# Expert result rows kept in DRAM and added once per token, and the next item's rows transposed inside the down product

## The reference, cut to what matters

```python
def moe_swiglu(a, router, w_gate, w_up, w_down):
    top_v, top_i = lax.top_k((a @ router).astype(jnp.float32), TOP_K)      # TOP_K = 2
    top_w = jax.nn.softmax(top_v, axis=-1)
    gate = jnp.sum(jax.nn.one_hot(top_i, N_EXPERTS) * top_w[..., None], axis=-2)
    out = jnp.zeros_like(a)
    for e in range(N_EXPERTS):                                            # 8
        h = jax.nn.silu(a @ w_gate[e]) * (a @ w_up[e])                    # 1024 -> 1408
        out = out + gate[..., e:e + 1] * (h @ w_down[e])                  # 1408 -> 1024
    return out
```

## Time and profile before

| | |
|---|---|
| median of 3 runs | 1282.21 us (1279.64 to 1285.29) |
| profiled execution | 1278.62 us, span 1276.7 us |
| PE busy | 1191.6 us, 93% of the span |
| DVE, ACT, POOL busy | 471.1, 282.0, 205.0 us |
| expert part | about 841 to 1240 us of the span |
| HBM read and written | 319.16 MB, 15.70 MB |

### The profile page before, as it was taken

How to read it: one execution, slowest core, us unless ns; L and a number is a source line. 1 busy time by engine, 2 the same in 40 slices (tenths; PEclk the granted TensorE clock), 3 DMA queues, 4 the chain that set the end, 5 groups by cost and what they waited for, 6 DMA issues and landing times.

```text
span 1276.7 us, 37806 instructions
## 1 busy us (share of the span) xinstructions
PE 1191.6 (93%) x15722; PEld 981.8 (77%) x15722; DVE 471.1 (37%) x1367; ACT 282.0 (22%) x757; POOL 205.0 (16%) x344
## 2 busy tenths in 40 slices
PE   7999999999999998998786879989899999999998
PEld 5887886999999976675344547787878977878976
DVE  2110114677774332003757674233211311212213
ACT  1000003110010022134867763121010110110122
POOL 3022132021340000223444541010000000000000
PEclk9999999999999998998989899999999999999999
DMA  9786869998443374564556876499999999989831
GB/s 308 294 321 244 316 242 336 152 392 306 139 159 116 149 280 149 169 105 132 182 178 222 263 232 237 158 387 385 399 363 379 360 360 379 349 341 380 318 124 37
DMA packets 109644, 330.06 MB, mean 259 GB/s; under 512 B 15816, under 2 KB 34201, under 8 KB 107812
## 3 DMA queue, kind: packets, MB, share of 16 engines
q1 hardware_dynamic: 91156, 263.86, 56.5%
q0 software_dynamic: 17168, 63.50, 16.3%
q10 hardware_dynamic: 1152, 0.30, 0.1%
HBM read 319.16 MB, written 15.70 MB: 262 GB/s over the span
## 4 chain that ended last, share of the span: by engine, by line
PE 86%; DVE 5%; issue 3%; ACT 2%; DMA 2%; POOLq 0%; POOL 0%; ACTq 0%; DVEq 0%
PE bank L1975 20%; PE bank L2591 15%; PE bank L2077 12%; PE pbank L2602 6%; PE bank L2113 6%; PE bank L2031 5%; PE pbank L2591 3%; PE bank L2602 3%; PE bank L2181 2%; DMA gring<-in_moe 1%; PE bank L2543 1%; PE bank L2208 1%; PE bank L2348 1%; PE bank L2303 1%; PE pbank L2543 1%
## 5 line engine op out<-in xcount | busy, mean ns | idle before, releaser
L2591 PE MATMUL bank<-X,gring 128*64 128x96 f32 x4608 | 197.0, 247 | 5.5 <-issue 5.5
L2591 PEld LDWEIGHTS bank<-X,gring 128*64 128x64 f32 x4608 | 193.0, 138 | 10.1 <-issue 10.1
L1975 PE MATMUL bank<-aT,gring 128*128 128x288 f32 x768 | 193.0, 410 | 3.5 <-DVE aT L1306 3.5
L1975 PEld LDWEIGHTS bank<-aT,gring 128*128 128x128 f32 x768 | 146.6, 192 | 46.2 <-issue 5.6
L2602 PE MATMUL pbank<-Q,X 128*32 128x256 f32 x1152 | 75.3, 379 | 0.0
L2077 PE MATMUL bank<-aT,gring 128*128 128x144 f32 x528 | 72.0, 286 | 0.0
L2031 PE MATMUL bank<-Q,X 128*64 128x64 f32 x2048 | 63.3, 223 | 7.7 <-issue 7.7
L2031 PEld LDWEIGHTS bank<-Q,X 128*64 128x64 f32 x2048 | 61.3, 138 | 11.7 <-issue 11.3
L1901 DVE TENSOR_TENSOR X<-X,bank 128x96 f32<-128x96 f32 x72 | 18.4, 256 | 134.5 <-ACT X L1252 132.6
L2077 PEld LDWEIGHTS bank<-aT,gring 128*128 128x128 f32 x528 | 67.7, 190 | 0.0
L1894 DVE TENSOR_TENSOR hT<-hT,bank 128x288 f32<-128x288 f32 x48 | 18.9, 448 | 128.5 <-PE bank L2543 128.5
(11 more groups left out here) (387 smaller groups left out, 1779.3 us busy)
## 6 DMA issues: line engine op xcount, KB each, us to landing
gring<-in_moe SPq DMA_DIRECT2D x176, 512.0 KB, 5.9
Q<-in_moe SPq DMA_DIRECT2D x72, 512.0 KB, 7.1
gring<-in_dense_gu SPq DMA_DIRECT2D x44, 512.0 KB, 14.1
Q<-in_cache_cmp POOLq DMA_DIRECT2D x64, 256.0 KB, 5.6
Q<-in_cache_cmp SPq DMA_DIRECT2D x64, 256.0 KB, 5.3
gring<-in_conv_in SPq DMA_DIRECT2D x24, 512.0 KB, 10.8
gring<-in_dense_down SPq DMA_DIRECT2D x16, 704.0 KB, 5.4
gring<-in_ple_gate SPq DMA_DIRECT2D x16, 512.0 KB, 6.2
```

Source lines behind the costliest of these rows:

```text
L1975: ins = pe.matmul(bank(label, k)[:, 0:T], tile[:, 128 * i:128 * i + 128], rhs[:, i, :], start=i == 0, stop=i == C - 1)
L2591: ins = pe.matmul(m_bank(i, M_GU + f)[64 * w:64 * w + 64, CAP * u:CAP * u + CAP], gslot(("m", 0), 2 * f + u)[:, o:o + 64], ae[:, c, :], st ...
```

## The change

The results of items 0 to 5 (`STORED` = 6) are no longer scattered by TensorE. After its three copies to `ye`, ACT's queue stores the 96 rows in a DRAM tensor `expert_rows` (four DMAs, 1 KB runs). Row 0 of that tensor is zero. In item 0, DVE works out for each token the two numbers of its rows and their gates (`out_numbers`). In item 6 POOL, once all stores have landed, fetches for each token its two rows (six indirect DMAs, 128, 128 and 32 tokens, two each); DVE multiplies by the gates and adds the two (`rows_added`, after parts 5, 7 and 9 of item 6's gate and up product); PE transposes the sums into 8 banks (`rows_transposed`, 24 transposes, between gate and up and down of item 6) and DVE adds them to `hT` (`sums_added`). The results of items 6 and 7 are scattered as before. Besides, the rows of items 1 to 6 are transposed after part 5 of the down product of the item before, and ACT copies them then.

```diff
+        expert_rows = nc.dram_tensor("expert_rows", (1 + STORED * CAP, D), f32, kind="Internal").ap()
 ...
 # POOL
+            pool.dma_start(expert_rows[0:1, :], atok[127:128, 2, :]).then_inc(slots_out, 16)
 ...
+            pool.wait_ge(slots_ready, 5)
+            m_full(pool, FIXED - 1, 1)
+            pool.wait_ge(stored, 16 * 4 * STORED)
+            for g in range(3):
+                n = 128 if g < 2 else 32
+                for k in range(2):
+                    pool.indirect_dma_start(rows_out[g][k][0:n, :], None, expert_rows[:, :],
+                                            bass.IndirectOffsetOnAxis(ap=out_index[0:n, 2 * g + k:2 * g + k + 1], axis=0)).then_inc(gathered[k], 16)
 # ACT
             def expert_acts(i):
+                if not isinstance(i, int) or i == 0:
+                    rows_loaded(i)
 ...
+                if isinstance(i, int) and i + 1 < FIXED:
+                    rows_loaded(i + 1)
                 for t in range(3):
                     m_full(act, i, M_DOWN + t)
+                    if t == 0 and isinstance(i, int) and i:
+                        act.wait_ge(stored, 16 * 4 * i)
                     m_drain(act.activation(ye[:, t, :], m_bank(i, M_DOWN + t)[:, 0:256], ACT.Copy), i, M_DOWN + t)
+            def rows_kept(i):
+                for t in range(3):
+                    m_drained(act, i, M_DOWN + t)
+                for j in range(4):
+                    dst = expert_rows[1 + CAP * i:1 + CAP * i + CAP, 256 * j:256 * j + 256]
+                    act.dma_start(dst.rearrange("(t r) n -> r t n", r=32), ye[32 * j:32 * j + 32, :, :]).then_inc(stored, 16)
 # DVE
+            def rows_added(g):
+                n = 128 if g < 2 else 32
+                a, b = rows_out[g]
+                for k in range(2):
+                    dve.wait_ge(gathered[k], 16 * (3 + 3))
+                chain(dve.tensor_scalar(a[0:n, :], a[0:n, :], out_gates[0:n, 2 * g:2 * g + 1], None, ALU.mult))
+                settled()
+                dve.scalar_tensor_tensor(a[0:n, :], b[0:n, :], out_gates[0:n, 2 * g + 1:2 * g + 2], a[0:n, :],
+                                         ALU.mult, ALU.add).then_inc(picks_ready, 1)
 ...
-                    if f == 5:
+                    if f == 5 and isinstance(i, int) and i == 0:
                         dve.wait_ge(slots_in, 16 * 2)
+                        row_numbers()
+                        out_numbers()
+                    if isinstance(i, int) and i == FIXED - 1 and f in (5, 7, 9):
+                        rows_added(f // 2 - 2)
+                    if f == 5 and not (isinstance(i, int) and i < STORED):
                         for t in range(3):
 ...
             for i in range(FIXED):
-                if i:
-                    expert_adds(i)
-                else:
-                    item_table()
                 expert_products(i, i, 0)
+            sums_added()
 # PE
-                if not (isinstance(i, int) and i == 0):
+                if not isinstance(i, int):
 ...
                     scatter(i)
 ...
+                if isinstance(i, int) and i == FIXED - 1:
+                    rows_transposed(i)
 ...
+                    if f == FC // 2 and isinstance(i, int) and i + 1 < FIXED:
+                        gathered_rows(i + 1)
```

More of the change, by code:

```diff
@@ L462, in m_place @@
         def m_place(i, k):
-            return k - C if isinstance(i, int) and i == 0 and k >= M_SCAT else k
+            if not isinstance(i, int):
+                return k
+            if k < M_SCAT:
+                return 2 * MB * i + k
+            first = 2 * MB * i + 2
+            if k < M_DOWN:
+                return first + k - M_GU
+            if k < M_SUM:
+                return first + FC + (C if i == FIXED - 1 else 0) + k - M_DOWN
+            return first + FC + k - M_SUM
         def m_turn(i, k):
             if isinstance(i, tuple):
-                return MR // MB * i[0] - 1
-            return m_place(i, k) // MB if isinstance(i, int) and i == 0 else MR // MB * i - 1 + k // MB
+                return MR // MB * i[0] + 1 - (MR // MB - 2) * FIXED
+            if isinstance(i, int):
+                return m_place(i, k) // MB
+            return MR // MB * i + 1 - (MR // MB - 2) * FIXED + k // MB
         m_base = RES[("pg", 1, 0)] - 2
@@ L1888, in row_numbers, with out_numbers @@
                 dve.tensor_copy(row_index[0:CAP, 1:FIXED], row_number[0:CAP, 1:FIXED]).then_inc(slots_ready, 1)
+            def out_numbers():
+                p1 = pos1[:, :, 0:STORED]
+                chain(dve.scalar_tensor_tensor(out_row, p1, float(CAP) + 0.5, p1, ALU.is_lt, ALU.mult))
+                settled()
+                chain(dve.scalar_tensor_tensor(out_hit, out_row, 0.0, first_row.unsqueeze(1).to_broadcast([128, 3, STORED]),
+                                               ALU.is_gt, ALU.mult))
+                settled()
+                chain(dve.tensor_tensor(out_row, out_row, out_hit, ALU.add))
+                settled()
+                chain(dve.tensor_reduce(out_sum, out_row, AX.X, ALU.add))
+                rows, gates = (t.rearrange("p (i k) -> p i k", k=2) for t in (out_rows, out_gates))
+                chain(dve.tensor_reduce(rows[:, :, 0], out_row, AX.X, ALU.max))
+                settled()
+                chain(dve.tensor_tensor(rows[:, :, 1], out_sum, rows[:, :, 0], ALU.subtract))
+                settled()
+                for k in range(2):
+                    chain(dve.tensor_tensor(out_hit, out_row, rows[:, :, k].unsqueeze(2).to_broadcast([128, 3, STORED]), ALU.is_equal))
+                    settled()
+                    chain(dve.tensor_tensor(out_hit, out_hit, rg[:, :, 0:STORED], ALU.mult))
+                    settled()
+                    chain(dve.tensor_reduce(gates[:, :, k], out_hit, AX.X, ALU.add))
+                    settled()
+                dve.tensor_copy(out_index[:, :], out_rows).then_inc(slots_ready, 1)
@@ L1890, in expert_adds, with sums_added @@
+            def sums_added():
+                i = FIXED - 1
+                for k in range(C):
+                    h = hT[:, scattered(k), :]
+                    m_full(dve, i, M_SUM + k)
+                    m_drain(dve.tensor_tensor(h, h, m_bank(i, M_SUM + k)[:, 0:T], ALU.add), i, M_SUM + k)
             def expert_adds(i):
@@ L2568, in picked_rows, with rows_transposed @@
                     m_fill(ins, i, h)
+            def rows_transposed(i):
+                pe.wait_ge(picks_ready, 6)
+                for k in range(C):
+                    m_free(pe, i, M_SUM + k)
+                    c = scattered(k)
+                    for g in range(3):
+                        n = 128 if g < 2 else 32
+                        ins = pe.transpose(m_bank(i, M_SUM + k)[:, 128 * g:128 * g + n], rows_out[g][0][0:n, 128 * c:128 * c + 128],
+                                           ident[0:n, 0:n])
+                    m_fill(ins, i, M_SUM + k)
             def expert_matmuls(i):
                 if not isinstance(i, int):
[L2572 to L2575, removed]
+                    picked_rows(i, i - FIXED + 2)
+                elif i == 0:
                     picked_rows(i, 0)
-                if not (isinstance(i, int) and i == 0):
+                if not isinstance(i, int):
                     for t in range(3):
                         m_drained(pe, i - 1, M_DOWN + t)
-                    pe.wait_ge(scat_ready, 3 * i)
+                    pe.wait_ge(scat_ready, 3 * i - 3 * STORED)
                     scatter(i)
@@ L2616, in _ @@
                 m_drained(pe, more + 1, M_DOWN + t)
-            pe.wait_ge(scat_ready, 3 * more + 6)
+            pe.wait_ge(scat_ready, 3 * more + 6 - 3 * STORED)
             scatter((more + 2,))
```

48 lines of the change are left out of this document (32 added, 16 removed).

## The result

The changed kernel takes 1289.86 us (median of 11 runs, 1287.18 to 1294.23) against 1282.43 us of the kernel before in the same comparison. The ratio is 1.0065, 95% interval 1.0045 to 1.0085: slower by 0.65%, some 8 us, where 4 us faster (no change that can be measured) was forecast. 1289.86 also lies above the stated range of 1264 to 1288. The profiled execution took 1289.68 us, 11.1 more than that of before.

A forecast was written before the change was run, and what follows sets the result against it. PE bounds the kernel now, DMA after the change: item 6 starts 16.2 us sooner, less 11.8 lost in it, 4.4 gained. The profiled 1278.6 becomes 1274.2, plus 3.6 to the median: 1277.8 us, range 1264 to 1288.

The forecast's parts named there:

- PE's side at the boundary: From down to the next gate and up: transposes move inside down, each boundary 3.3 us shorter, 19.8 us at six.
- item 0's row numbers: DVE's added `out_numbers` in item 0, 3.4 us, makes things 1.3 us later but is covered, so costs nothing.
- T + 38.2: Item 6, T being its start at 1125.1: time at which DVE has the sums of the fetched rows ready.
- DMA then sets the period, and the boundary time that PE no longer spends comes back in part as waits for ring tiles: Items 2 to 5: DMA needs 46.3 us an item, against 44.2 for PE alone.
- as long as before: Item 7 and the end: no change in length, so the 4.4 us gained by down of item 6 stays.
- 24 transposes take 2.8: Item 6, between PE's wait of 9.0 us for the sums and down: transposing the sums takes 2.8 us.
- D: Rival: item 6's fetch lands over 14.4 us after its last issue; with 25 us, 1293 us; chance 0.11.
- E: Rival: bandwidth already binds the items' periods, so added stores and fetch make it 13 us slower, 1295; chance 0.07.
- C: Rival: DMA is the bound at 47.7 us an item; the change moves the wait, gain -1.2, 1283 us; chance 0.22.

The follow-up runs named there:

- experiments 4 to 6: Weight loads of items 1 to 7 narrowed: to a quarter, kernel before 1268.9 us, changed kernel 1254.8; to three quarters, changed kernel, periods of items 2 to 5 44.5 us.
- experiment 8: Changed kernel with 14 useless products on TensorE ahead of its wait for the sums in item 6: ratio 1.0050 to the kernel before.

## Why the prediction was wrong

**Right.** PE's side at the boundary: down, with the transposes in it, runs straight into gate and up, and TensorE alone saves 3.0 us an item (forecast 3.3). The 0.3 us of idle time that the forecast saw ahead of the transposes isn't there: in the kernel before they start at 1137.39 on the chain, where down's last product ends. Nothing done for ACT, DVE or item 0's row numbers shows on the chain. In item 6 the chain of steps held as a whole: sums at T + 38.0 (forecast T + 38.2), though by parts that differ. The stores had landed at T + 7.9, not T + 12.2, and the last fetch took 13.3 us, not 10.

**The step that failed first: "DMA then sets the period, and the boundary time that PE no longer spends comes back in part as waits for ring tiles".** About half came back, and not as that. From gate and up 0 to gate and up 6 TensorE alone gains 17.3 us (the two kernels with a quarter of the loads). Item 6 started 9.6 us sooner relative to item 0, where 16.2 were forecast. The first four periods were 48.2, 47.8, 48.5 and 48.1 where 46.3 was forecast, with pauses at "issue" of some 2.5 us an item, and the fifth 45.1. What held them was code that arrived late, and not tiles (experiments 4 to 6). Only 2.7 us of waits for weight tiles occur, in item 0. The short pauses were in the trace of the kernel before, four of them in item 1, where the queues were fullest (one stands in the earlier trace rows), and the prediction took them as a leftover of item 1 that fades. They were the sign of what happens when the queues have no pause. The forecast also had no term for them in items 2 to 5 and none in item 7, which it left "as long as before": that was 4.1 us more.

**The step that failed second: "24 transposes take 2.8".** They took 7.0, and down 1.6 more than usual. The forecast had PE idle for 9 us and gave it the full clock after that. Of these 5.8 us 4.2 belong to the clock (2.6 in the transposes, 1.6 in down, experiment 8) and 1.6 to the three shapes in turn; the row used had two, one after the other. Gate and up of item 6 took 1.8 longer than forecast and the wait 2.0 less.

**The rivals.** D, a late fetch, did not happen: the fetch was on time. Its 1293 lies nearest to the measured time, by chance. E is out: 388 GB/s over 240 us, without a wait for a tile in that stretch. C comes nearest in what happened, with periods over 47 and "moves the wait", though with another wait than it named, and its 1283 is 7 us short.

Together: -9.6 instead of -16.2 is 6.6, item 6 costs 15.8 instead of 11.8, 4.0, and what follows 5.7 instead of 0. Of these 16.3 us the two profiled executions show 15.5 between 4.4 faster and 11.1 slower. The medians show 8 slower, so a part of the last terms is particular to that execution.

## What to carry to other kernels

Where the queues are nearly full, time in which an engine asks for nothing is not free to take away: look at what else uses it, and count short pauses without a named cause as a load that will grow, above all in a long unrolled program. Whether they are waits for instructions shows in two things, the number of records between them (256 of matmuls and weight loads here) and the start of the instruction queue's packets. Before moving a step out of a boundary, look for the wait that it fills there, here ACT's copies. A wait on TensorE can cost more than its length: behind those of 4.0 and 7.0 us here the work started at half the clock, and behind two of six of 2.4 us. And a detour over DRAM has to be cheap at the moment when it comes, which three different places for the fetch here were not.

## What the runs showed of the hardware

- TensorE waited for instructions at block edges of 256 records, mostly 0.6 to 1.0 us, 16 times in 240 us at 388 GB/s and share 1.01 of all queues, 8 times at 368 and 0.97, never in 220 us at 312 and 0.95. It went on 2.2 to 2.7 us after the 16 KB packet started.
- After 7.0 us without work TensorE was granted 0.50, 1.2 GHz, for the next 7 us of transposes, and 2.4 GHz again by 1180. It was at 0.50 after 4.0 us without work too, and at 0.56 to 0.59 for 3 us after two of six waits of 2.43 us.
- In the changed kernel six indirect fetches of up to 128 rows of 4 KB, issued 1.25 us apart, landed 8.3 to 13.4 us after their issue. In two of four kernels with full weight loads TensorE went on at 1 to 5 matmuls in 0.7 to 1.4 us meanwhile.
- Transposes of 128, 128 and 32 rows in turn take 0.55 us a group of three; grouped by shape, 0.33 for three.
